# One wide high-weight product for both parts of the activation in the 256-token down products and output projections, with the bank's halves added at the drain

## What is computed

```python
h = h + concat([y_r, y_n]) @ w_out                            # first block, 256 tokens
h = h + (silu(xn @ w_gate) * (xn @ w_up)) @ w_down            # first block, D_FF = 2816

for l in range(2):                                            # second block
    h_x = h_x + 0.5 * gate * swiglu(..., ffn1_up[l], ffn1_down[l])     # h_c likewise: 512 tokens
    h_x = h_x + mod_x[:, :, 5] * (concat([o_a, o_b, o_c]) @ w_out[l])  # 512 tokens for l = 0
    h_x = h_x + 0.5 * gate * swiglu(..., ffn2_up[l], ffn2_down[l])     # 512 tokens for l = 0
    # for l = 1 the context is no longer needed here: w_out and ffn2 see 256 tokens
return rmsnorm(h_x)
```

## Time and profile before

| what | value |
|---|---|
| median of 3 runs | 2228.96 us (2226.67 to 2229.51) |
| span of the profiled execution | 2226.0 us |
| ScalarE busy | 770.7 us, 35% |
| TensorE products on 256 tokens with ff_hi or ff_lo as activation | 1056 |
| TensorE products on 256 tokens at lines 458 to 460, other activations | 2760 |
| mean granted TensorE clock | 0.974 |

### The profile page before, as it was taken

One profiled execution on the slowest core, in us unless ns is written; L12 is line 12 of the kernel. 1 busy time (PEld: TensorE's weight loads), 2 busy tenths in 40 slices (PEclk: granted clock), 3 DMA queues, 4 the chain that ended last, 5 costly groups with the idle time before them and its releaser, 6 DMA issues. The chain is left out here.

```text
span 2226.0 us, 40781 instructions
## 1 busy us (share of the span) xinstructions
PE 2133.4 (96%) x17742; PEld 1835.3 (82%) x17742; DVE 1074.6 (48%) x1570; ACT 770.7 (35%) x1094; POOL 60.2 (3%) x59
## 2 busy tenths in 40 slices
PE   7997799999999999989999999999999999899998
PEld 7886599997888887867778888878888888779998
DVE  5654665555333334576453333354333335755555
ACT  5431444443221233236342222233222223355443
POOL 0000030000000000120000000000000000200000
PEclk9998899998999999999999999999999999999999
DMA  7516654543423314428522232232232225254553
GB/s 282 199 61 228 217 187 166 200 161 114 165 78 117 104 65 136 93 96 287 188 95 89 91 113 94 78 139 76 78 116 99 83 94 155 95 194 159 174 178 110
DMA packets 56626, 303.56 MB, mean 136 GB/s; under 512 B 13728, under 2 KB 17184, under 8 KB 27552
## 3 DMA queue, kind: packets, MB, share of 16 engines
q1 hardware_dynamic: 56480, 301.40, 39.8%
HBM read 300.33 MB, written 1.05 MB: 135 GB/s over the span
## 5 line engine op out<-in xcount | busy, mean ns | idle before, releaser
L458 PE MATMUL ps<-a_hi,w_hi 128*128 128x512 f32 (+1 forms) x1992 | 684.3, 344 | 1.7 <-DVE w_lo L445 1.6
L459 PE MATMUL ps<-a_lo,w_hi 128*128 128x512 f32 (+1 forms) x1992 | 678.4, 341 | 0.0
L460 PE MATMUL ps<-a_hi,w_lo 128*128 128x512 f32 (+1 forms) x1992 | 678.0, 340 | 0.0
L445 DVE TENSOR_TENSOR w_lo<-raw,w_hi 128x2048 fp32r<-128x2048 f32 (+2 forms) x230 | 470.3, 2048 | 216.3 <-ACT w_hi L439 216.0
L439 ACT ACTIVATE w_hi<-raw 128x2048 fp32r<-128x2048 f32 (+2 forms) x229 | 391.2, 1715 | 242.8 <-PE ps L460 174.3
L458 PEld LDWEIGHTS ps<-a_hi,w_hi 128*128 128x128 f32 x1992 | 378.0, 190 | 48.7 <-issue 3.7
L460 PEld LDWEIGHTS ps<-a_hi,w_lo 128*128 128x128 f32 x1992 | 378.2, 190 | 42.1
L459 PEld LDWEIGHTS ps<-a_lo,w_hi 128*128 128x128 f32 x1992 | 378.3, 190 | 41.6
L458 PE MATMUL ps<-ff_hi,w_hi 128*128 128x512 f32 (+1 forms) x880 | 306.5, 348 | 3.8 <-DVE w_lo L445 3.8
L459 PE MATMUL ps<-ff_lo,w_hi 128*128 128x512 f32 (+1 forms) x880 | 304.9, 347 | 0.0
L460 PE MATMUL ps<-ff_hi,w_lo 128*128 128x512 f32 (+1 forms) x880 | 304.9, 346 | 0.0
(11 more groups left out here) (354 smaller groups left out, 1796.6 us busy)
## 6 DMA issues: line engine op xcount, KB each, us to landing
raw<-in_w_gu SPq DMA_DIRECT2D x110, 1024.0 KB, 4.8
raw<-in_w_ada SPq DMA_DIRECT2D x72, 1024.0 KB, 5.2
raw<-in_w_dn SPq DMA_DIRECT2D x80, 704.0 KB, 4.1
raw<-in_w_in SPq DMA_DIRECT2D x26, 1024.0 KB, 5.2
raw<-in_w_out SPq DMA_DIRECT2D x12, 1024.0 KB, 4.9
direct<-in_w_cmp SPq DMA_DIRECT2D x4, 1024.0 KB, 7.0
h<-in_x SPq DMA_DIRECT2D x2, 1024.0 KB, 7.1
nb<-in_rpb SPq DMA_DIRECT2D x32, 64.0 KB, 7.2
```

The source lines that it names most:

```text
L445: nc.vector.tensor_tensor(w_lo[slot][:, cols], raw[b][:, cols], w_hi[slot][:, cols].bitcast(F32), ALU.subtract).then_inc(lo_ready if done ...
L458: nc.tensor.matmul(banks[m], w1, a1, start=start and k == 0, stop=False)
L459: nc.tensor.matmul(banks[m], w1, a2, start=False, stop=False)
L460: last = nc.tensor.matmul(banks[m], w2, a1, start=False, stop=stop and k == pr.kt - 1)
```

## The change

In the down products and output projections on 256 tokens, the two products with the high weight become one. Its moving operand is both parts of the activation, 2 x 256 columns, and it fills the whole bank: the left half gets high times high, the right half high times low. The product with the low weight stays and adds to the left half. The drain of each output tile becomes two instructions: the first adds the right half to h, the second, which waits on VectorE for the first, adds the left half. For this the two parts of an activation lie in one tensor.

```diff
-    a_hi = place("a_hi", [P, KT, T2], F32R)
-    a_lo = place("a_lo", [P, KT, T2], F32R)
+    a_both = place("a_both", [P, 2, KT, T2], F32R)
+    a_hi, a_lo = a_both[:, 0], a_both[:, 1]
     at_f = cursor[0]
-    ff_hi = place("ff_hi", [P, FH, T2], F32R)
-    ff_lo = place("ff_lo", [P, FH, T2], F32R)
+    ff_both = place("ff_both", [P, 2, FH, T2], F32R)
+    ff_hi, ff_lo = ff_both[:, 0], ff_both[:, 1]
...
+    half_added = sem("half_added")
...
+    PAIRED = ("down", "res")
+    def paired(pr):
+        return pr.kind in PAIRED and pr.tokens == S
+    def halves_added(pr):
+        return sum(p.n * p.mt for p in products if paired(p) and p.kind != "gu" and p.base < pr.base)
...
+                if paired(pr):
+                    nc.tensor.matmul(in_halves(banks[m]), w1, both(k), start=k == 0, stop=False)
+                    last = nc.tensor.matmul(banks[m][:, 0:S], w2, a1, start=False, stop=k == pr.kt - 1)
+                    continue
...
+    def in_halves(b):
+        return b.rearrange("p (a t) -> p a t", a=2)
...
+            both = lambda k: ff_both[:, :, k, 0:t]
         else:
             rhs = lambda k: (a_hi[:, k, 0:t], a_lo[:, k, 0:t])
+            both = lambda k: a_both[:, :, k, 0:t]
...
                 elif gate is None:
                     hk = h[:, bass.ds(j, 1), 0:t]
+                    if paired(pr):
+                        nc.vector.tensor_tensor(hk, one(b[:, S:T2]), hk, ALU.add).then_inc(half_added, 1)
+                        dve.wait_ge(half_added, halves_added(pr) + j + 1)
                     last = nc.vector.tensor_tensor(hk, one(b[:, 0:t]), hk, ALU.add)
                 else:
                     for w in range(t // S):
                         hk = h[:, bass.ds(j, 1), w * S:(w + 1) * S]
+                        if paired(pr):
+                            nc.vector.scalar_tensor_tensor(hk, one(b[:, S:T2]), gate(j, w), hk, ALU.mult,
+                                                           ALU.add).then_inc(half_added, 1)
+                            dve.wait_ge(half_added, halves_added(pr) + j + 1)
                         last = nc.vector.scalar_tensor_tensor(hk, one(b[:, w * S:(w + 1) * S]),
                                                               gate(j, w), hk, ALU.mult, ALU.add)
```

More of the change, by code:

```diff
@@ L446, in split_lo, with multiply @@
                                 ALU.subtract).then_inc(lo_ready if done is None else done, 1)
-    def multiply(pe, pr, c, slot, banks, lhs, rhs, start=True, stop=True, before=None):
+    PAIRED = ("down", "res")
[3 more added lines that the diff above has]
+        return sum(p.n * p.mt for p in products if paired(p) and p.kind != "gu" and p.base < pr.base)
+    def multiply(pe, pr, c, slot, banks, lhs, rhs, both=None, before=None):
         pe.wait_ge(lo_ready, c + 1)
@@ L457, in multiply @@
                 a1, a2 = rhs(k)
-                nc.tensor.matmul(banks[m], w1, a1, start=start and k == 0, stop=False)
+                if paired(pr):
+                    nc.tensor.matmul(in_halves(banks[m]), w1, both(k), start=k == 0, stop=False)
+                    last = nc.tensor.matmul(banks[m][:, 0:S], w2, a1, start=False, stop=k == pr.kt - 1)
+                    continue
+                nc.tensor.matmul(banks[m], w1, a1, start=k == 0, stop=False)
                 nc.tensor.matmul(banks[m], w1, a2, start=False, stop=False)
-                last = nc.tensor.matmul(banks[m], w2, a1, start=False, stop=stop and k == pr.kt - 1)
+                last = nc.tensor.matmul(banks[m], w2, a1, start=False, stop=k == pr.kt - 1)
         last.then_inc(chunk_mult, 1)
@@ L604, in body @@
                 multiply_ada(pe, pr.loaded(first + k, 0, 1), ps[6][:, 0:64])
-            multiply(pe, pr, c, slot, [bank(slot, m, t) for m in range(pr.mt)], lhs, rhs, before=before)
+            multiply(pe, pr, c, slot, [bank(slot, m, T2 if paired(pr) else t) for m in range(pr.mt)], lhs, rhs, both, before)
         if pr.kind in ("down", "res"):
```

## The result

The changed kernel takes 2233.86 us (median of 5 runs, 2232.61 to 2236.94), the kernel before on the same chip 2227.72 us (5 runs, 2224.3 to 2229.51). The ratio of the runs is 1.0039, 95% interval [1.0023, 1.0055]: 0.4% slower, some 8.7 us (5.1 to 12.3). The medians lie 6.1 us apart, within that interval. The forecast was 2237.5 us from a median of 2228.96, a ratio of 1.0038.

The account below looks back on a forecast made before the run. TensorE bounds A1 and A2; a VectorE drain ring bounds B1, B2, P1 and P2. 3.46 + 3.94 + 1.74 + 1.53 - 2.10 = +8.57 us on 2228.96 gives 2237.5 us, range 2232.5 to 2241.5.

Parts of the forecast that it names:

- TensorE's gain per chunk: Wide products save each tile's fixed part: 0.150 us per down chunk, 0.218 per projection chunk, down chunks at 3.81 us.
- rival of a dearer wide product: The two-piece operand costs as much as two products, so TensorE's work isn't shortened: +12.2 us, 2241.1 us; chance 10%.
- A1 and A2: 256-token down products without squares, bound by TensorE: 7 chunks each 0.150 us shorter, added drains covered, 2.10 us gained together.
- The addition's price: Each output tile's extra drain instruction on VectorE, wait included: 0.46 us without a gate, 0.52 with one.
- P2: 256-token output projection with gated drains, bound by the ring: 8 x 0.52 us added, first chunk 0.22 shorter, +3.94.
- upper bound: Added drains on VectorE with a 0.11 us gap, 0.1 more in loops of A1, A2 and B2: +11.2, 2240.2 us.
- the ring: Drain, squares, high split, low split over VectorE and ScalarE; bounds B1, B2, P1 and P2, so added drains lengthen it.
- P1: 256-token output projection with ungated drains, bound by the ring: 8 x 0.46 = 3.68 us added, first chunk 0.22 shorter, +3.46.
- The rival that one of them doesn't end with its last drain: P1 or P2 ends with something else, such as a w_ada load, covering additions in part: +4, 2233 us; chance 9%.
- B1: 256-token down product with squares, ungated drains: ring 4.12 to 4.58 us, five steps 1.28 slower, +1.74 in all.
- 1.63 us of slack: At B1's end, the last drain's squares wait behind the w_ada chunk, so the last two drains' 0.92 us add nothing.
- B2: 256-token down product with squares, gated drains: six steps 27.06 against 25.90 us, last drain's addition open, +1.53 in all.

Follow-up runs that it names:

- early high split alone: Kernel before, with ScalarE's high split of the next but one chunk put ahead of the squares in B1 and B2: ratio 0.9949, measured again 0.9979.
- drain half alone: Kernel before, with each output tile of the change drained by two dependent additions, the high-weight products kept separate at 256 wide: ratio 1.0052.

## Why the prediction was right

**TensorE's gain per chunk**: right, 3.81 us where 3.81 was forecast, and a wide product of two pieces takes 0.23 us to the next start, so that the rival of a dearer wide product falls. A1 and A2 gave 1.98 of 2.10 us.

**The Trainium skill's 2.5 ns per product** (TensorE: Matmul & The Clock Gate, "Wait — 56ns, not 53.3ns?") would have left an estimated 0.03 us a chunk to gain; the chunks got 0.15 shorter, or 0.07 in the slower of the two paces below. The measurement decides for the rows.

**The addition's price**: 0.45 and 0.51 to 0.52 us where 0.46 and 0.52 were taken. The Trainium skill's rule that a semaphore between VectorE's operations costs nothing (VectorE: DVE Perf Modes, "The DRAIN you can't avoid") does not hold here: two waits less in a drain of P2 made it 0.25 us shorter. The upper bound's gap of 0.11 us and its 0.1 us more for a count computed from the loop's register stand in none of the rows; in A2's loop the second addition starts 0.52 us behind the first, in P2, written out, 0.51.

**P2**: +4.15 against 4.16, the ring as forecast. **P1**: the mechanism was right and the size off, +2.86 against 3.68. The step that failed is the one that costs P1 by its additions alone, as if the splits kept their duration: with GpSimd squaring the context beside them the four splits last 1.6 us longer before and 1.0 us after. Without that work it is +3.47. In both projections the forecast 0.22 us for the first chunk came to 0.09. The rival that one of them doesn't end with its last drain falls: before and after, the columns of squares behind both wait for ScalarE's squares of the last chunk. What the forecast put at nothing is the start of the norm behind them, 0.30 and 0.36 us later in this profile, where TensorE's granted clock was lower.

**B1**: steps of 4.57 to 4.58 as forecast, and the w_ada load was issued 27.55 us after the first drain instead of 25.86, +1.69. The step that failed is that the last drain had 1.63 us of slack behind this load. In the profile of before its product started 6.27 us after the load's issue, in the changed kernel 4.94, and the columns of squares waited for ScalarE:

```profile
505.00 1.10 PE L506 MATMUL ps<-raw,silu_c 128*32 128x64 f32 x64 [0.83 <-DMA raw<-in_w_ada]
...
508.76 1.87 PE L953 MATMUL ps<-consts_sb,gu 128*128 128x1 f32 x8 [1.22 <-ACT gu L724]
```

So the last drain decides when the load is quick. The kernel with the change in A1 and A2 only has the ring of before in B1 and a quick load (4.87 us); there the columns start 33.64 us after the first drain. Against that the change adds 2.6 us to B1, the 1.69 and the 0.92 of the last two drains; against the profile of before 1.0. With 2.6 the stages would sum to +9.2 us instead of +7.6.

That this is no matter of the kernel is shown by the two profiles of the early high split alone. Timeline, the product with w_ada in the first and in the second of them, each with a window over TensorE's work behind it, 7.3 and 7.4 us long (the third number from the end of a window's row is the granted clock):

```profile
503.72 1.10 PE L487 MATMUL ps<-raw,silu_c 128*32 128x64 f32 x64 [0.77 <-DMA raw<-in_w_ada]
```

```profile
503.70:511.00 7.30, 5.13 (x90) 4.25 (x90) 3.82 (x10) 3.61 (x8) 0.00 (x0) 0.87 0.90 348
```

```profile
504.65 1.94 PE L487 MATMUL ps<-raw,silu_c 128*32 128x64 f32 x64 [2.11 <-DMA raw<-in_w_ada]
```

```profile
504.60:512.00 7.40, 6.65 (x86) 6.36 (x86) 0.91 (x5) 1.08 (x3) 0.00 (x0) 0.50 0.76 292
```

One program: the product started 5.1 us after the load's issue in the first and 6.4 in the second; TensorE idled for 0.77 and 2.11 us, and after the longer pause it ran at a granted clock of 0.50, its lower level of 1.2 GHz, so that the same 64 products took 1.94 instead of 1.10 us and the columns came 34.87 instead of 31.60 us after the first drain. The pause alone doesn't decide this: after 2.03 us of it in the kernel before, and after 2.46 in the drain half alone, the same 64 products took 1.10 us. Why the load takes 5 or 6.4 us in one place was not tried.

**B2**: +1.75 against 1.53; the six steps took 27.20 instead of 27.06 and the last one was shortened by 0.06, not 0.15.

The forecast sum was +8.57, the stages give +7.6 and the ratio 8.7 (5.1 to 12.3). That the total fits better than its parts is chance.

## What to carry to other kernels

The share of busy time (96% against 48%) said that this change pays; the rows of each stage said where it does. In P1 and P2, where hardly a drain behind the first waits for TensorE, an addition to the drain cost its full duration, and TensorE's gain was lost. In B1 and B2, where TensorE was late in every second step, it first used up that lateness: five additions of 0.45 us made B1's five steps 1.2 us longer. Where every drain waits for TensorE, the trade pays as long as VectorE's idle time there stays well above what is added. And before something is added to a ring, look for what need not be in it: the high split ahead of the squares took 4.2 us out of B1 and B2, the wide product 1.4 to 2 us out of A1 and A2 (the ratios of the two, 0.9979 and 0.9981, don't rank them).

## What the hardware showed beyond that

Stages with a wide and a narrow product in turn ran at one of two paces in A1 and A2, 3.81 or 3.88 us a chunk, the same for a whole stage: in the kernel with the change in A1 and A2 only, 3.88 in A1 and 3.81 in A2, at a granted clock of 1.00 in both windows. The full change had 3.81 in both, the kernel without the added additions 3.88 in both. In P1 and P2 the full change ran at the slower pace, 0.353 us for a wide and a narrow product against 0.347 in A1 and A2, and their first chunks gained 0.09 us and not 0.22. Stages with one width alone kept one pace in every profile, 3.96 us for 256 and 7.48 for 512 columns. What sets the pace stays open.

Kernels whose work is the same up to P1's end had its first drain at 275.86 to 283.18 us, 7.3 us apart, with a granted clock between 0.88 and 0.95 from 110 to 270 us: more than any stage of this change. Only the same stage of both, or many runs, can be compared.
